# A two-layer transformer stack on one core: modulation vectors made in jobs of two half blocks, with the first projection begun between two jobs

## The reference

```python
'ada_w': nrm((DEPTH, D, 6 * D), 0.5 * D ** -0.5),      # DEPTH 2, D 1024

def norm_modulate(h, g, shift, scale):
    return rms_norm(h, g) * (1 + scale) + shift

def gqa_mixer(hx, hc, w_in, q_g, k_g, w_out, ctx_out):
    ...
    def project(h):
        q, k, v = jnp.split(h @ w_in, splits, axis=-1)
```

## Time and profile before

| | |
|---|---|
| Time, median of 3 runs (range) | 2109.2 us (2107.32 to 2110.25) |
| Profiled execution, first to last instruction (span) | 2097.7 us |
| PE busy | 1967.4 us, 94% |
| DVE, ACT, POOL busy | 63%, 51%, 13% |
| Chain that ended last | PE 82%, DVE 8%, ACT 4%, issue 3%, POOL 2%, DMA 1% |
| Mean granted TensorE clock | 0.963 |
| HBM read | 361.57 MB |

### The profile page before, as it was taken

One profiled execution on the slowest core, in us unless ns is written; L12 is line 12 of the kernel. 1 busy time (PEld: TensorE's weight loads), 2 busy tenths in 40 slices (PEclk: granted clock), 3 DMA queues, 4 the chain that ended last, 5 costly groups with the idle time before them and its releaser, 6 DMA issues.

```text
span 2097.7 us, 32755 instructions
## 1 busy us (share of the span) xinstructions
PE 1967.4 (94%) x13464; PEld 1692.6 (81%) x13464; DVE 1320.6 (63%) x1986; ACT 1068.7 (51%) x1724; POOL 281.6 (13%) x291
## 2 busy tenths in 40 slices
PE   5999989999999899999999888999898899999998
PEld 2775668888778776899988888999886788888886
DVE  3238545777454568577546555444566688888886
ACT  3246533333334476566446425444435477676774
POOL 1201132011100301322012312111100000000000
PEclk9999999999999899999999999999998999999998
DMA  8232442554222221255543013545451388979784
GB/s 337 105 137 102 161 179 103 181 199 181 101 81 101 87 81 41 101 181 183 214 146 141 22 42 137 186 172 201 149 213 65 149 344 320 350 302 354 305 345 159
DMA packets 52668, 364.81 MB, mean 174 GB/s; under 512 B 5920, under 2 KB 8224, under 8 KB 8864
## 3 DMA queue, kind: packets, MB, share of 16 engines
q1 hardware_dynamic: 50016, 357.59, 45.9%
q10 hardware_dynamic: 2496, 5.05, 0.7%
HBM read 361.57 MB, written 1.05 MB: 173 GB/s over the span
## 4 chain that ended last, share of the span: by engine, by line
PE 82%; DVE 8%; ACT 4%; issue 3%; POOL 2%; DMA 1%; DVEq 0%; POOLq 0%; ACTq 0%; SPq 0%
PE ps L77 22%; PE ps L78 21%; PE ps L79 21%; PE ps L74 15%; DVE WLO L91 3%; PE ps L82 2%; ACT R L85 2%; ACT WHI L85 1%; DVE SM L105 1%; POOL R L91 1%; DVE R L91 1%; DMA ring<-W 1%; POOL h L95 0%; DVE x L88 0%; DVE h L88 0%
## 5 line engine op out<-in xcount | busy, mean ns | idle before, releaser
L91 DVE TENSOR_TENSOR WLO<-ring,WHI 128x1024 fp32r<-128x1024 f32 x566 | 683.4, 1243 | 218.4 <-ACT WHI L85 218.0
L85 ACT ACTIVATE WHI<-ring 128x1024 fp32r<-128x1024 f32 x566 | 577.5, 1053 | 121.9 <-PE ps L79 120.0
L77 PE MATMUL ps<-HHI,WHI 128*128 128x256 f32 (+1 forms) x1680 | 546.4, 325 | 30.4 <-DVE HLO L88 15.0
L78 PE MATMUL ps<-HLO,WHI 128*128 128x256 f32 (+1 forms) x1744 | 558.5, 320 | 0.0
L79 PE MATMUL ps<-HHI,WLO 128*128 128x256 f32 (+1 forms) x1680 | 539.6, 321 | 0.0
L77 PEld LDWEIGHTS ps<-HHI,WHI 128*128 128x128 f32 x1680 | 328.8, 196 | 69.2 <-issue 38.0
L78 PEld LDWEIGHTS ps<-HLO,WHI 128*128 128x128 f32 x1744 | 341.4, 196 | 20.0
L79 PEld LDWEIGHTS ps<-HHI,WLO 128*128 128x128 f32 x1680 | 328.7, 196 | 21.3
L74 PE MATMUL ps<-R 64*64 64x64 f32 (+10 forms) x2448 | 190.6, 289 | 4.1 <-ACT R L85 2.0
L85 ACT ACTIVATE R<-ps,VEC 128x512 f32<-128x512 f32 (+1 forms) x106 | 69.3, 659 | 242.3 <-PE ps L79 240.2
L91 POOL TENSOR_TENSOR R<-R 128x256 f32<-128x256 f32 (+1 forms) x99 | 106.4, 1078 | 554.6 <-ACT R L85 554.2
(11 more groups left out here) (208 smaller groups left out, 2852.6 us busy)
## 6 DMA issues: line engine op xcount, KB each, us to landing
ring<-W SPq DMA_DIRECT2D x340, 1024.0 KB, 4.9
x<-xt ACTq DMA_DIRECT2D x1, 2048.0 KB, 14.6
out<-x SPq DMA_DIRECT2D x2, 512.0 KB, 4.0
CR<-const_nsa ACTq DMA_DIRECT2D x1, 560.0 KB, 4.7
CR<-const_rw ACTq DMA_DIRECT2D x1, 448.0 KB, 3.4
CR<-const_gqa ACTq DMA_DIRECT2D x1, 320.0 KB, 17.0
CR<-const_mla ACTq DMA_DIRECT2D x1, 320.0 KB, 2.9
VEC<-vec ACTq DMA_DIRECT2D x1, 314.0 KB, 17.4
```

The costliest lines, as they stand in the source:

```text
L77: self.e.matmul(out, l[0], r[0], start=start, stop=False)
L78: self.e.matmul(out, l[0], r[1], start=False, stop=False)
L85: return self.e.activation(out, in_, func, **kw)
L91: return self.e.tensor_tensor(out, in0, in1, op)
```

## The change

1. A *job* takes the place of a vector: two blocks of 512 features each (`JOBS`). `job_step` puts four k tiles x 512 features of one block into a chunk; steps 0 and 1 are the first block, 2 and 3 the second. Each of the four products of a step goes to its own band kk. `SCP` grows to 34 columns with silu(c) in columns 2 and 3: read from column 2 the result lies in rows 0 and 1 of a band, read from column 0 in rows 2 and 3, with zeros added to the others. So one copy to `EV` holds both blocks, and the turn is 4 products with four columns (`ROWS4`). `ada_job_dve` writes MOD and GS in halves.
2. Job 0 is the first 512 features of shift and scale, job 1 the second 512. Jobs 2 to 7 are the same vectors as before. The chunks now come as: job 0 (4), units 0 and 1 of the first projection (1), job 1 (4), units 2 and 3 (1).
3. PE runs job 0 with the sum of squares and the spread inside it, its turn, and starts the block: k = 0, steps 0 and 1 of job 1, k = 1, step 2, k = 2, step 3, k = 3, the turn of job 1, k = 4 to 7. ACT and DVE split their work at k = 3 in the same way (`second_job`). The bank of the spread is kept out of the ring until the turn of job 1.
4. x comes in two transfers of 1 MB issued by SP ahead of the chunks.

```diff
@@ Feed.begin @@
-        for _ in range(UNITS):
+        for i in range(UNITS):
+            if between and i == 2:
+                between()
             self.st.first += self.unit()
@@ layout @@
+JOBS = [((0, 0, half), (0, 1, half)) for half in range(2)]
+JOBS += [((layer, m, 0), (layer, m, 1)) for layer, ms in ((0, (2, 3, 4, 5)), (1, (0, 1))) for m in ms]
+    def job_step(n, s):
+        layer, m, half = JOBS[n][s // 2]
+        F.fresh()
+        out = [F.wt("ada_w", (layer,), 4 * (s % 2) + kk, m * 1024 + 512 * half, 512) for kk in range(4)]
+        F.fresh()
+        return out
-    L["ada_pe"] = [ada_step(0, (0, 1), s) for s in range(8)]
-    st = L["gqa_in"] = F.begin(12)
+    L["ada_pe"] = [job_step(0, s) for s in range(4)]
+    st = L["gqa_in"] = F.begin(12, lambda: L["ada_pe"].extend([job_step(1, s) for s in range(4)]))
...
@@ first_squares_act @@
-        a.wait_ge(*at("d_x"))
         for q in range(4):
+            a.wait_ge(*at("d_x%d" % (q // 2)))
@@ ada_part_pe @@
+        first = 2 - 2 * (s // 2)
         for kk, p in enumerate(pieces):
-            for half in range(2):
-                o = 32 * (2 * half + kk)
-                i = pe.mm(b[o:o + 32, :], SCP[:, 2 * s + kk, :], raw_of(p)[:, 512 * half:512 * half + 512], s == 0, s == 3)
+            i = pe.mm(b[32 * kk:32 * kk + 32, :], SCP[:, 4 * (s % 2) + kk, first:first + 32], raw_of(p), s == 0, s == 3)
@@ ada_turn_pe @@
-        for j in range(8):
-            half = j // 4
-            i = pe.mm(b[:, 2 * j:2 * j + 2], EV[:, 128 * (j % 4):128 * (j % 4) + 128], PARTS[:, 2 * half:2 * half + 2],
-                      True, True)
+        for j in range(4):
+            i = pe.mm(b[:, 4 * j:4 * j + 4], EV[:, 128 * j:128 * j + 128], ROWS4, True, True)
+    def ada_job_dve(v, n):
...
+        for i, (layer, m, half) in enumerate(JOBS[n]):
+            t = v.tt(o, rows[:, :, 2 * i:2 * i + 2], col3(VEC[:, adab:adab + 4], 2), ALU.add)
...
+        for layer, m, half in JOBS[n]:
+            if m in (1, 4):
+                v.wait_ge(*last("mod"))
+                v.stt(go, o, 1.0, col3(VEC[:, gb:gb + 4], 2), ALU.add, ALU.mult).then_inc(*did("mod", ("gains", layer, m, half)))
@@ gqa_pe @@
+        def second_job(k):
+            for s in {1: (0, 1), 2: (2,), 3: (3,)}.get(k, ()):
+                ada_part_pe(pe, L["ada_pe"][4 + s], 1, s)
+            if k == 4:
+                ada_turn_pe(pe, 1)
+                give(bank_of["rs", 0])
+        project_block(pe, st, [(("gq", m), ("gsq", m), 512, hx(0, 512)) for m in GQA_ORDER[:4]], normed(0), second_job)
@@ tensor @@
         for s in range(4):
             ada_part_pe(pe, L["ada_pe"][s], 0, s)
-        for s in range(4):
-            ada_part_pe(pe, L["ada_pe"][4 + s], 1, s)
-            if s == 0:
-                ada_turn_pe(pe, 0)
             if s == 1:
                 first_sum_pe(pe)
-        spread_pe(pe, 0)
-        ada_turn_pe(pe, 1)
+            if s == 2:
+                spread_pe(pe, 0)
+                keep(bank_of["rs", 0])
+        ada_turn_pe(pe, 0)
         gqa_pe(pe)
@@ scalar @@
-        load(a, x[:, :, :], xt_in, "d_x")
...
+        root_act(a, 0)
         ada_row_act(a, 0, None)
-        root_act(a, 0)
-        ada_row_act(a, 1, 0)
-        hi_units(a, L["gqa_in"].first)
-        apply_act(a, 0)
+        hi_units(a, L["gqa_in"].first[0:2])
+        def second_job(k):
+            if k == 3:
+                ada_row_act(a, 1, 0)
+                hi_units(a, L["gqa_in"].first[2:4])
+        apply_act(a, 0, second_job)
@@ vector @@
+        def second_job(k):
+            if k == 3:
+                v.wait_ge(*at("mod0", 0, 0))
+                ada_job_dve(v, 1)
+                lo_units(v, L["gqa_in"].first[2:4])
+                v.wait_ge(*at("mod", 0, 1))
+        lo_units(v, L["gqa_in"].first[0:2])
+        apply_dve(v, 0, [("mod", 0, 0)], second_job)
@@ sync @@
+        for i in range(2):
+            load(s, x[:, 4 * i:4 * i + 4, :], xt_in[:, 4 * i:4 * i + 4, :], "d_x%d" % i)
         load_chunks(s, 0, L["cut", 0])
```

More of the change, by code:

```diff
@@ L163, in fresh, with begin @@
         self.fill = SLOT
-    def begin(self, units):
+    def begin(self, units, between=None):
         self.fresh()
         self.st, self.left, self.opened, self.own = Stream(), units, 0, []
-        for _ in range(UNITS):
+        for i in range(UNITS):
+            if between and i == 2:
+                between()
             self.st.first += self.unit()
@@ L248, in consts @@
         c0[:, 387 + half], c0[:, 389 + half] = (p // 64 == half) / 64, p // 64 == half
-        for part in range(2):
-            c0[:, 391 + 2 * part + half] = (p % 32 == half) & (p // 64 == part)
+    for row in range(4):
+        c0[:, 391 + row] = p % 32 == row
     def perm(pairs, n=128):
@@ L380, in layout @@
     for m in GQA_ORDER[4:]:
-        steps.append(ada_step(0, (2, 3, 4, 5), len(steps)))
+        steps.append(job_step(2 + len(steps) // 4, len(steps) % 4))
         F.group([("gqa_w_in", (0,), k, 128 * m, 128) for k in range(8)])
@@ L385, in layout @@
     for s in (6, 7):
-        steps.append(ada_step(0, (2, 3, 4, 5), s))
-    L["ada1_pe"] = [ada_step(1, (0, 1), s) for s in range(8)]
+        steps.append(job_step(3, s - 4))
+    L["ada1_pe"] = [job_step(6 + s // 4, s % 4) for s in range(8)]
     st = L["gqa_out"] = F.begin(8)
     for j in range(8):
-        steps.append(ada_step(0, (2, 3, 4, 5), 8 + j))
+        steps.append(job_step(4 + j // 4, j % 4))
         F.group([("gqa_w_out", (0,), k, j * 128, 128) for k in range(8)])
@@ L565, in program @@
     GSS = sb("GS", 64)[:, :].rearrange("p (l a n) -> p l a n", l=2, a=2)
-    SC, SCP, SM = sb("SC", 16), sb("SCP", 256)[:, :].rearrange("p (k n) -> p k n", n=32), sb("SM", 320)
+    SC, SCP, SM = sb("SC", 16), sb("SCP", 272)[:, :].rearrange("p (k n) -> p k n", n=34), sb("SM", 320)
     GF = sb("GF", 24)
@@ L597, in program @@
     MEANS = {1024: C0[:, 384:385], 384: C0[:, 385:386], 256: C0[:, 386:387]}
-    HALF_MEAN, HALF_SUM, PARTS = C0[:, 387:389], C0[:, 389:391], C0[:, 391:395]
+    HALF_MEAN, HALF_SUM, ROWS4 = C0[:, 387:389], C0[:, 389:391], C0[:, 391:395]
     SQ = R2[:, 11264:12288].rearrange("p (a n) -> p a n", a=2)
@@ L1036, in ada_turn_pe @@
         pe.wait_ge(*at("d_c0"))
-        for j in range(8):
-            half = j // 4
-            i = pe.mm(b[:, 2 * j:2 * j + 2], EV[:, 128 * (j % 4):128 * (j % 4) + 128], PARTS[:, 2 * half:2 * half + 2],
-                      True, True)
+        for j in range(4):
+            i = pe.mm(b[:, 4 * j:4 * j + 4], EV[:, 128 * j:128 * j + 128], ROWS4, True, True)
         i.then_inc(*did("group", ("ada_sum", n // 6, n % 6)))
+    def ada_job_dve(v, n):
+        rows = bank("ada", n // 6, n % 6)[:, 0:16].rearrange("p (j r) -> p j r", r=4)
+        v.wait_ge(*at("ada_sum", n // 6, n % 6))
+        v.wait_ge(*at("d_vec"))
+        for i, (layer, m, half) in enumerate(JOBS[n]):
+            o = MOD[:, layer, 16 * m + 8 * half:16 * m + 8 * half + 8].rearrange("p (j s) -> p j s", s=2)
+            adab = vcols["ada_b", (layer,)] + 8 * m + 4 * half
+            t = v.tt(o, rows[:, :, 2 * i:2 * i + 2], col3(VEC[:, adab:adab + 4], 2), ALU.add)
+        t.then_inc(*did("mod", ("mod0", n // 6, n % 6)))
+        last_mod = ("mod0", n // 6, n % 6)
+        for layer, m, half in JOBS[n]:
+            if m in (1, 4):
+                gb = vcols["norm1_g" if m == 1 else "norm2_g", (layer,)] + 4 * half
+                go = GSS[:, layer, 0 if m == 1 else 1, 8 * half:8 * half + 8].rearrange("p (j s) -> p j s", s=2)
+                o = MOD[:, layer, 16 * m + 8 * half:16 * m + 8 * half + 8].rearrange("p (j s) -> p j s", s=2)
+                v.wait_ge(*last("mod"))
+                v.stt(go, o, 1.0, col3(VEC[:, gb:gb + 4], 2), ALU.add, ALU.mult).then_inc(*did("mod", ("gains", layer, m, half)))
+                last_mod = ("gains", layer, m, half)
+        S.events["mod", n // 6, n % 6] = S.events[last_mod]
     ADA1, ACC = (2, 3, 4, 5), R2[:, 4096:6144].rearrange("p (v n) -> p v n", v=2)
@@ L1521, in gqa_pe @@
         st, steps = L["gqa_in"], L["ada0"]
-        project_block(pe, st, [(("gq", m), ("gsq", m), 512, hx(0, 512)) for m in GQA_ORDER[:4]], normed(0))
+        def second_job(k):
[5 more added lines that the diff above has]
+        project_block(pe, st, [(("gq", m), ("gsq", m), 512, hx(0, 512)) for m in GQA_ORDER[:4]], normed(0), second_job)
         after = [[(gqa_sum_pe, 8), (gqa_sum_pe, 9), (gqa_sum_pe, 0), (gqa_sum_pe, 1), (gqa_rope_pe, 0), (gqa_rope_pe, 1)],
@@ L1616, in gqa_dve @@
             if t == 5:
-                ada_out_dve(v, 0, 2)
+                ada_job_dve(v, 2)
         lo_units(v, st.ahead[10])
@@ L3532, in last_recip_dve @@
         v.recip(RT[:, 0:2], ROOT[:, 0:2]).then_inc(*did("recip"))
-    mod_norm(0, 0, 0, 0, 512, lambda k: [("d_x",)])
+    mod_norm(0, 0, 0, 0, 512, lambda k: [("d_x%d" % (k // 4),)])
     mod_norm(1, 0, 1, 0, 512, xed("gqa_out"), 7)
@@ L3681, in vector @@
         v.wait_ge(*at("silu_c"))
```

(15 more changed lines are left out.)

## The result

The changed kernel takes 2091.3 us (median of 5 runs, 2088.94 to 2097.81) against 2107.32 (median of 5, 2102.21 to 2110.25). The ratio is 0.9941, 95% interval 0.9925 to 0.9957: about 12 us faster. One execution on record, of a kernel with a pad of 32 bytes (e12), took 6628 us where its other nine took 2100 to 2104, and is left out.

A forecast was written before the change was run, and what follows sets the result against it. The prediction took PE to bound the kernel, busy 94% of the span, except where it waits. A start gain of 1.6 us plus 5.6 from later turns gave 7.2, so 2109.2 - 7.2 = 2102.0 us, range 2098.0 to 2107.5.

The forecast's parts named there:

- Time until the block: Kernel start up to the block's first product: claimed to end at 32.0 us, 14.2 earlier than before.
- The block: First projection's 96 products with job 1 inside: claimed to end at 68.3 us, against 69.85 before.
- the wait in the middle: PE idle between job 1's turn and k = 4, for MOD, GS and WLO: claimed 5.4 us.
- The start's gain: Gain read when PE has finished the block: claimed 1.6 us, between 0.2 and 2.6.
- the mark: The moment PE has finished the block, where the start is read: 69.85 us before, 68.3 forecast.
- The later turns: Six turns of jobs 2 to 7 lose 8 of 16 records: claimed 0.93 us each, 5.6 in all.
- the larger SCP are nothing: Side term in the later turns: two more small stores and the larger SCP were claimed to cost nothing.
- The base: Unchanged kernel's time: span 2097.7 plus 11.5 us around it, 2109.2, from which the gain was subtracted.
- The third, full clock earlier: Rival: PE reaches 2.4 GHz ahead of the block, so spread, step 3 and turn 0 halve: 2.6 us more, 2099.4; chance 0.12.
- the fourth: Rival: the clock doesn't rise in the block's first half, net +5.0 us, 2114.2; chance 0.06.
- the clock's case: The rival with full clock earlier, which with a short start set the range's lower end, 2098.0 us.

The follow-up runs named there:

- e12: Changed kernel with SM 312 columns wide, so ring, WHI and WLO lie 32 bytes further than in the kernel before; ratio 0.9985 to the kernel before.
- e8: Changed kernel run again with no edit, in a later session; ratio 0.9931 to the kernel before.
- e15: Changed kernel run a third time with no new edit; ratio 0.9917 to the kernel before, median 2087.3 us.
- e1: Kernel before run again with no edit; ratio 1.0002 to the kernel before.
- e3: Changed kernel with SM 16 columns narrower, so ring, WHI and WLO lie where they lay before; ratio 0.9964 to the kernel before.
- e11: Changed kernel with SM 368 columns wide, so ring, WHI and WLO lie 256 bytes further than before; ratio 0.9953 to the kernel before.
- e4: Changed kernel's jobs, turns and addresses, but both jobs ahead of an uninterrupted block and x again as ACT's transfers; ratio 0.9932 to the kernel before.
- e2: Kernel before with SM 16 columns wider, so ring, WHI and WLO lie 64 bytes further; ratio 0.9984 to the kernel before.
- e5: Kernel before with 16 idle columns between ring and WHI, so only WHI and WLO move by 64 bytes; ratio 0.9970.
- e13: Kernel before with 16 idle columns ahead of the first tile, so every SBUF tile moves by 64 bytes; ratio 1.0009.
- e7: Kernel before with SM 32 columns wider, so everything behind it moves by 128 bytes; ratio 1.0056.

## Why the prediction was wrong

- *Time until the block.* Forecast 32.0, measured 31.63 (31.98 and 32.05 in the other profiles). Chunk 1 let PE begin at 15.43 (15.0 forecast); step 3 ended at 24.6 (24.1), the turn took 1.05 rather than 1.8, since PE had full clock by then. The spread took 2.01 from start to start for 1.55: the 1.55 in the earlier trace rows was no price of the slow clock, since TensorE sped up inside that spread (its records follow each other in 0.214 us and then in 0.111). Right in sum, by misses that cancel.
- *The block.* End of k = 3 at 48.6 (49.3), the wait in the middle 5.21 (5.4), the end at 68.34 (68.3). No step waited for a chunk. Right, and two terms were mis-sized again in opposite directions: dense products at 0.233 instead of 0.227, and the first start slow for 6 products only. That the end came out at 68.3 is in part luck: in e8 and e15 the same program has 68.75 and 69.10, with 6 to 9 slow products at each start.
- *The start's gain,* 1.6 forecast: 1.5 by the mark, from one execution of each. The mark itself scatters with the slow products: at the old paces it is 69.85 and 70.93 (e1) without the change, 69.46 (e3) and 69.97 (e11) with it. And e4 shows no part of the new order in it: with both jobs ahead the block ends at the same time within this scatter. The 12 us won ahead of the block are given back inside it, 5.2 as the wait, the rest as steps that had stood in front, the turn and the second slow start. What the mark gained is of the size of the two cheaper turns. The prediction had listed these terms and drawn no such conclusion.
- *The later turns.* Forecast 0.93 each; 0.88 measured at the one in the attention. At the old addresses (e3) the whole change is worth 7.6 us (4.6 to 10.7), the mark some 1.5, which leaves about 6 for six turns. Right as far as this interval tells, and measured singly at one turn only.
- *The failed step* is one half sentence: "the larger SCP are nothing". This term of the sum, put at zero with no regard to what lies behind SCP, is worth 5 to 10 us. The 16 columns are no work, but they moved WHI and WLO by 64 bytes against the tiles ahead of them, the moving operands among these, and the dense stages run at another pace. Shown by e2, e3, e5 and e13. Its size is what separates e3 (0.9964) from the changed kernel (0.9917 to 0.9941): 5 to 10 us across sessions, 6.7 between e3 and e4 in one session, and 3.4 and 6.3 us when done to the kernel before (e2, e5). Whether it is worth more in the changed kernel than in the one before can't be told within these intervals. It costs time where products have 512 columns and gives more where they have 256.
- *The base.* I put 11.5 us around the span. The executions list 1.8. The rest was the scatter between one quick execution and the median; this shifted no difference, but a forecast of 2102.0 stands on a median of 2109.2 that five runs put at 2107.3 and the later sessions at 2102.8 to 2105.5. The absolute time is off by that too, the gain isn't.
- *Rivals.* The third, full clock earlier, came true in part: the clock had risen by the time of the turn, which gave some 1.0 of the 2.6 us it was priced at (step 3 took 1.67 for 1.94, the turn 1.05 for 1.8), and nothing in the spread. The clock did rise in the first half, which rules out the fourth. None named the layout, and the range had its lower end at the clock's case.

Open: why the distance sets the pace, and from which tile it counts. The intervals are 0.2269, 0.2333 and between for 512 columns, 0.1133, 0.1178 and 0.1200 for 256. The runs show that a relative shift of WHI and WLO does it, the shifts that do, and the values, not the place where it is decided. Nor do they show why one program has 0.1178 in some executions and 0.1133 in others in the same stage.

## What to carry to other kernels

When a tile's size changes, look at what is allocated behind it: a few idle columns made this kernel of dense products up to 0.3% faster (e5) or 0.6% slower (e7), as much as a reordering that took much thought. Measure a change once with the old addresses restored by an unused gap, or its gain is mixed with that of the layout. And moving work from ahead of a block to its middle gains only what the block doesn't wait for there; compare it with the plain order before crediting it.

## What the runs showed of the hardware

- The dense float32 products in three passes have a pace that depends on how far their stationary operand lies in SBUF from tiles ahead of it, the moving operand among them. A shift by 256 bytes gives the old pace back, shifts by 32, 64, 128 and 192 don't. At PEclk 1.00 and PE busy throughout it is 835 (before) to 885 (e8) products of 256 columns in 100 us.
- One program spans 2097.7 and 2105.9 us in two executions (kernel before and e1) at equal pace. The granted clock differs, 0.963 and 0.952: 3.6 of the 8.2 us are lost from 100 to 200 us (PEclk 0.98 and 0.93), 3.3 from 550 to 750 (0.96 and 0.94), and nothing to speak of behind 900.
- A start after idle time ran slow for 6 (changed kernel, k = 0), 8 (the same, k = 4), 9 (before) and 12 (e4) products of 512 columns; at 0.2 us each that is 1.2 to 2.4 us. The Trainium skill (TensorE: Matmul & The Clock Gate, The HAM clock gate) says this number varies from run to run; the trace agrees.
- The Trainium skill (TensorE: Matmul & The Clock Gate, The HAM clock gate) gives 0.2157 us from start to start for back-to-back products of 512 columns at full clock. These products, each with a stationary operand of its own to load, don't reach it: their quickest pace here is 0.2269 (kernel before, 350 to 540 us).
